# Attention probabilities: scaled with queries on the partitions and transposed, instead of scored a second time transposed

## What is computed

```python
s = jnp.einsum('bqkgd,blkd->bkgql', qblk, k).astype(jnp.float32)
if sink is not None:
    s = jnp.concatenate([s, col], axis=-1)       # one sink logit per head
p = jax.nn.softmax(s, axis=-1)
if sink is not None:
    p = p[..., :-1]
return jnp.einsum('bkgql,blkd->bqkgd', p.astype(v.dtype), v)
```

## Time and profile before

| what | value |
|---|---|
| median of 3 runs | 1517.91 us (1515.63 to 1521.51) |
| profiled execution, its time | 1520.94 us |
| its span (first to last instruction) | 1519.1 us |
| mean granted clock of TensorE | 0.986 |
| TensorE busy | 1445.8 us, 95% |
| VectorE / GpSimd / ScalarE busy | 796.1 / 771.7 / 587.9 us (52 / 51 / 39%) |

### The profile page before, as it was taken

The page is one execution under the profiler, slowest core; times in us unless marked ns, Lnnn a source line. Parts: engine busy times, 40 slices in busy tenths (PEclk is TensorE's granted clock), DMA queues, the critical chain, the costliest instruction groups (busy, mean ns, idle before and its releaser), DMA issues.

```text
span 1519.1 us, 21747 instructions
## 1 busy us (share of the span) xinstructions
PE 1445.8 (95%) x8776; PEld 1306.1 (86%) x8776; DVE 796.1 (52%) x1164; ACT 587.9 (39%) x934; POOL 771.7 (51%) x554
## 2 busy tenths in 40 slices
PE   5999999999998999999979999998999999999996
PEld 3898889889887888999868988897988879999985
DVE  4675676452677520312784747764436775022157
ACT  4334564233764311213243346542357632222140
POOL 2454676323676443344674557753246755443443
PEclk9999999999999999999999999999999999999998
DMA  8412000212000443444320220012110013215221
GB/s 336 126 56 74 29 28 21 90 47 83 28 29 28 132 156 122 141 159 139 124 98 28 88 70 15 29 56 73 56 57 28 29 53 113 76 62 198 96 99 70
DMA packets 36756, 126.90 MB, mean 84 GB/s; under 512 B 5040, under 2 KB 5680, under 8 KB 36656
## 3 DMA queue, kind: packets, MB, share of 16 engines
q1 hardware_dynamic: 29952, 108.54, 21.3%
q10 hardware_dynamic: 6704, 16.97, 3.1%
HBM read 119.73 MB, written 5.77 MB: 83 GB/s over the span
## 4 chain that ended last, share of the span: by engine, by line
PE 87%; DVE 5%; POOL 3%; issue 2%; ACT 2%; DVEq 0%; POOLq 0%; ACTq 0%
PE ps L910 46%; PE ps L858 7%; PE ps L860 7%; PE ps L859 7%; PE ps L1045 3%; PE ps L1043 2%; PE ps L1095 2%; PE ps L1072 2%; PE ps L1071 2%; PE ps L1092 2%; PE ps L1093 2%; PE ps L927 1%; POOL w_lo L1764 1%; DVE o_inv L1633 1%; PE ps L1102 1%
## 5 line engine op out<-in xcount | busy, mean ns | idle before, releaser
L1764 POOL TENSOR_TENSOR w_lo<-raw,w_hi 128x1024 fp32r<-128x1024 f32 x148 | 360.1, 2440 | 359.0 <-ACT w_hi L1138 358.7
L910 PE MATMUL ps<-h_hi,w_hi 128*128 128x320 f32 x1280 | 299.3, 315 | 18.4 <-DVE g_c L1645 8.0
L910 PE MATMUL ps<-h_hi,w_lo 128*128 128x320 f32 x1280 | 292.6, 310 | 0.0
L910 PE MATMUL ps<-h_lo,w_hi 128*128 128x320 f32 x1280 | 292.6, 310 | 0.0
L1792 POOL TENSOR_TENSOR p_lo<-p_f,p_hi 128x512 fp32r<-128x512 f32 x164 | 211.9, 1296 | 139.0 <-ACT p_hi L1298 138.2
L910 PEld LDWEIGHTS ps<-h_hi,w_hi 128*128 128x128 f32 x1280 | 217.3, 189 | 39.3 <-DVE g_c L1645 9.8
L910 PEld LDWEIGHTS ps<-h_lo,w_hi 128*128 128x128 f32 x1280 | 215.9, 189 | 2.2
L910 PEld LDWEIGHTS ps<-h_hi,w_lo 128*128 128x128 f32 x1280 | 215.6, 189 | 2.2
L1138 ACT ACTIVATE w_hi<-raw 128x1024 fp32r<-128x1024 f32 x148 | 152.8, 1051 | 92.1 <-DMA raw<-in_weights 53.7
L1589 DVE TENSOR_REDUCE top<-ps 128x1 f32<-128x512 f32 (+1 forms) x128 | 83.7, 658 | 144.7 <-PE ps L1050 105.0
L1660 DVE TENSOR_TENSOR gy<-ps,sg 128x640 f32<-128x640 f32 x32 | 26.4, 824 | 241.2 <-PE ps L910 241.1
(11 more groups left out here) (180 smaller groups left out, 2599.2 us busy)
## 6 DMA issues: line engine op xcount, KB each, us to landing
raw<-in_weights SPq DMA_DIRECT2D x190, 512.0 KB, 3.4
raw_more<-in_weights SPq DMA_DIRECT2D x10, 512.0 KB, 10.6
x<-in_x_sample ACTq DMA_DIRECT2D x6, 512.0 KB, 8.0
x_mid<-x ACTq DMA_DIRECT2D x5, 512.0 KB, 2.6
x<-x_mid ACTq DMA_DIRECT2D x5, 512.0 KB, 6.5
y_sample<-x SPq DMA_DIRECT2D x3, 512.0 KB, 2.6
pack<-in_pack ACTq DMA_DIRECT2D x2, 528.0 KB, 4.8
x<-in_x_sample SPq DMA_DIRECT2D x2, 512.0 KB, 4.9
```

The lines of the kernel that those rows point to most:

```text
L910: last = pe.matmul(ps[:, s + half, 0:HALF], w[:, u % RING, cols], acts[:, k, half * HALF:(half + 1) * HALF], start=k == 0 and part == 0, s ...
L1764: did(pool.tensor_tensor(w_lo[:, n % RING, :], raw_tile(r), w_hi[:, n % RING, :], ALU.subtract), w_ready)
```

## The change

- The transposed scores, the `row` transposes, `q_m`, the ones rows and the sink's slots and products go.
- `S` stays. When VectorE has a head's maximum it writes at once the negated maximum, joined with the cache's maximum or the sink (`neg`), and a new entry `ex` on ScalarE exponentiates that head's scores from the score bank into `p_f` in SBUF, with the sum of the row taken by the same instruction. The bank is free after `ex`, no longer after the maximum. In A the cached keys' scores are first copied to SBUF (`cached`).
- A new entry `iv` on VectorE adds the partial sums, takes the reciprocal of 128x4 and scales each head's probabilities in place.
- `T` replaces `ST`: TensorE transposes four 128x128 blocks of the scaled probabilities into one bank; ScalarE copies them out rounded (`p_hi`), and VectorE subtracts straight from PSUM (`pl`, formerly GpSimd's).
- `PV` is two products: the value operand holds high and low values side by side, and meets `p_hi` and `p_low`. `O` adds both halves: ScalarE copies the lower half out, VectorE adds.
- `attention` gets a first filler, put between the first scores: z1 and gate b3, which used to be made ahead of the stage. `lag` is 2 instead of 3. Scores of group g begin with the last step of group g - 2, since `p_f` has two buffers, and `iv` comes two steps ahead of the group's first transposes. `with_splits` places no split between a group's last score and its `iv`.
- `zeros` (one memset) takes the place of `ones`.

```diff
-def attention(l, br, filler, last_filler, lag, row_ahead, score_ahead):
+def attention(l, br, first_filler, filler, last_filler, lag, ahead):
...
+        holder = p_place(g)[2]
+        start = -1 if holder < 0 else first[holder + 1] - 1
+        end = max(first[g] - ahead, start)
         for i, e in enumerate(units):
-            early[start + (end - start) * (i + 1) // len(units)].append(e)
+            at = start + (end - start + 1) * i // len(units)
+            scores[at].append(e)
+            exps[at].append(("ex", *e[1:]))
+        inverses[end if end < 0 else end + 1].append(("iv", l, br, g))
...
     for n, (g, i) in enumerate(steps):
-        out.append(("ST", l, br, g, i))
-        out.extend(early[n])
+        out.append(("T", l, br, g, i))
+        out.extend(scores[n])
+        out.append(("pl", l, br, g, i))
         tick()
         if n >= lag:
             product(n - lag)
         fill()
+        out.extend(inverses[n])
+        out.extend(exps[n])
...
-    out.extend(flat(attention(l, "a", filler[:-5], filler[-5:], 3, 2, 4)))
+    out.extend(flat(attention(l, "a", filler[:8], filler[8:-5], filler[-5:], 2, 3)))
...
-    out.extend(flat(attention(l, "b", filler[:-3], filler[-3:], 3, 2, 4)))
+    out.extend(flat(attention(l, "b", filler[:6], filler[6:-3], filler[-3:], 2, 3)))
...
+        if e[0] == "S" and e[4] == len(score_units(*e[2:4])) - 1:
+            held = True
+        if e[0] == "iv":
+            held = False
...
-            while started and turn in due and due[turn] <= 0 and not (freed[turn - RING][:2] == ("oc", 0)):
+            while started and not held and turn in due and due[turn] <= 0 and not (freed[turn - RING][:2] == ("oc", 0)):
...
+                    elif kind == "T":
+                        _, l, br, g, i = e
                         s = begin(e)
+                        n = NO[("iv",) + e[1:4]]
+                        pe.wait_ge(over_sum, n + 1)
+                        for h in range(GRP):
+                            last = pe.transpose(ps[:, s, h * P:(h + 1) * P], p_part(br, g)[:, h, i * P:(i + 1) * P], ident)
                         did(last, filled[s])
...
+                        n = NO[("T",) + e[1:]]
+                        wait_drained(pe, ("T",) + e[1:])
+                        values = vv[:, key, kv, :, :].rearrange("p s d -> p (s d)")
+                        pe.matmul(ps[:, b, :], values, p_hi[:, n % 3, :], start=i == 0, stop=False)
+                        last = pe.matmul(ps[:, b, :], values, p_low(br, n), start=False, stop=ends)
...
+                        for h in range(GRP) if unit == "heads" else (unit,):
+                            p, bias = p_part(br, g)[:, h, :], neg[:, c % 3, h:h + 1]
+                            if br == "a" and unit != "heads":
+                                wait_drained(act, ("S", l, br, g, 0))
+                                act.activation(p[:, LAT * P:], cached[:, g % 2, h * P:(h + 1) * P], ACT.Exp, bias=bias,
+                                               accum_out=sums[:, c % 3, 1, h:h + 1])
+                                p = p[:, 0:LAT * P]
+                            n = p.shape[-1]
+                            src = ps[:, s, h * P:(h + 1) * P] if unit == "heads" else ps[:, s, 0:n]
+                            last = act.activation(p, src, ACT.Exp, bias=bias, accum_out=sums[:, c % 3, 0, h:h + 1])
+                        did(last, drained[s])
...
+                            after(did(dve.tensor_reduce(best[:, h:h + 1], ps[:, s, 0:n * P], axis=AX.X, op=ALU.max)))
+                            other = others[:, h:h + 1] if br == "a" else sinks[:, h:h + 1]
+                            did(dve.tensor_scalar(neg[:, c, h:h + 1], best[:, h:h + 1], other, -1.0, ALU.max, ALU.mult), neg_made)
...
+                        wait_drained(dve, ("S", l, br, g, len(score_units(br, g)) - 1))
+                        total = sums[:, c, 0, :]
+                        if br == "b" or GROUPS[g][1]:
+                            after(did(dve.tensor_tensor(total, total, sums[:, c, 1, :], ALU.add)))
+                        after(did(dve.reciprocal(inv[:, c, :], total)))
+                        for h in range(GRP):
+                            part = p_part(br, g)[:, h, :]
+                            last = dve.tensor_scalar(part, part, inv[:, c, h:h + 1], None, ALU.mult)
+                        did(last, over_sum)
+                    elif kind == "pl":
+                        _, l, br, g, i = e
+                        n, s = NO[e], PLACE[("T",) + e[1:]][0]
+                        dve.wait_ge(p_hi_made, n + 1)
+                        did(dve.tensor_tensor(p_low(br, n), ps[:, s, :], p_hi[:, n % 3, :], ALU.subtract), drained[s])
```

More of the change, by code:

```diff
@@ L42 @@
 FRONT = 0
-TOP_ROW = 96
 HF_ACT = 4
@@ L52, with group_slots, p_place @@
 FIRST_MODS = (0, 4, 1, 5, 2, 6, 3, 7)
-def key_slots(br, tile):
-    last = [(SINK, None)] if br == "b" else []
+def group_slots(br, g):
+    tile = GROUPS[g][1]
     if tile == 0:
-        return [(0, None)] + last
+        return [0]
     if br == "a":
[L62 to L68, removed]
+        return [1, 2, 3, 4, CACHE]
+    return {1: [CACHE, 1, 2], 2: [CACHE, 1, 2, 3], 3: [2, 3, 4, CACHE], 4: [3, 4, CACHE]}[tile]
+def p_place(g):
+    return (g % 2, 0, g - 2) if g < 2 * T - 2 else (0, g - (2 * T - 2), 2 * T - 4)
 def score_units(br, g):
@@ L102, in attention @@
     first = [steps.index((g, 0)) for g in range(count)]
-    early = {n: [] for n in range(-1, len(steps))}
-    start = -1
+    scores = {n: [] for n in range(-1, len(steps))}
+    exps = {n: [] for n in range(-1, len(steps))}
+    inverses = {n: [] for n in range(-1, len(steps))}
     for g in range(count):
         units = [("S", l, br, g, u) for u in range(len(score_units(br, g)))]
-        end = max(first[g] - score_ahead, -1)
+        holder = p_place(g)[2]
+        start = -1 if holder < 0 else first[holder + 1] - 1
+        end = max(first[g] - ahead, start)
         for i, e in enumerate(units):
-            early[start + (end - start) * (i + 1) // len(units)].append(e)
[L110 to L115, removed]
+            at = start + (end - start + 1) * i // len(units)
+            assert at >= -1 and (holder < 0 or at >= first[holder + 1] - 1)
+            scores[at].append(e)
+            exps[at].append(("ex", *e[1:]))
+        inverses[end if end < 0 else end + 1].append(("iv", l, br, g))
     filler = list(filler)
-    places = len(steps) + len(early[-1])
+    places = len(steps)
     out, later, used = [], [], [0, 0]
@@ L289, in layer_order @@
                 ("qt", l, "b", 0)])
-    for c in range(KT_B):
+    for c in range(KT_B - 1):
         out.extend(whole(gate("b", c)))
@@ L293, in layer_order @@
     filler = []
-    for br in "cu":
-        for c in range(KT_B):
-            filler.extend(chunks(gate(br, c), 6))
-            filler[-1] = (filler[-1], gate(br, c))
-    out.extend(flat(attention(l, "b", filler[:-3], filler[-3:], 3, 2, 4)))
+    for br, c in [("b", KT_B - 1), *((br, c) for br in "cu" for c in range(KT_B))]:
+        filler.extend(chunks(gate(br, c), 6))
+        filler[-1] = (filler[-1], gate(br, c))
+    out.extend(flat(attention(l, "b", filler[:6], filler[6:-3], filler[-3:], 2, 3)))
     out.append(("pool", 0, 1, 2, 3, 4, 5, 6, 7))
@@ L393, in with_splits @@
 def with_splits(order, freed, lag):
-    count, out, due, turn, started = len(freed), [], {}, RING, False
+    count, out, due, turn, started, held = len(freed), [], {}, RING, False, False
     for e in order:
@@ L586 @@
 V_HI, O_MADE, O_DONE, MOD_USER = counts()
-ROWS = [e for e in ORDER if e[0] == "row"]
-O_STAGES = [e[:4] for e in ORDER if e[0] == "O" and e[4] == 0]
+NEG_NO = {}
+for _e in [e for e in ORDER if e[0] == "S"]:
+    NEG_NO[_e] = len(NEG_NO) + 1
+ES_NO = {}
+for _e in [e for e in ORDER if e[0] == "S" and e[2] == "b" and score_units(*e[2:4])[e[4]] in ("heads", GRP - 1)]:
+    ES_NO[_e] = len(ES_NO) + 1
+O_STAGES = [e for e in ORDER if e[0] == "O"]
 O_PER_LAYER = len(O_DONE) // DEPTH
@@ L1634, in _ @@
                         for odd in range(2):
[L1635 to L1638 removed]
+                            dve.wait_ge(o_low_made, 2 * n + odd + 1)
+                            half = og_sum(n)[head_rows(odd), :, :]
@@ L1639, in _ @@
+                            last = dve.tensor_tensor(half, by_head(ps[0:HD, b, :])[:, odd:GRP:2, :], half, ALU.add)
+                            did(last, drained[b] if odd else None)
                     elif kind == "gT" and e[2] == "u":
```

279 lines of the change are left out of this document (103 added, 176 removed).

## The result

The changed kernel takes 1553.15 us (median of 4 runs, 1551.52 to 1554.89); the kernel before took 1518.42 beside it (4 runs). The ratio is 1.0228, with a 95% interval of 1.0205 to 1.0251: 35 us slower, where 45 faster was forecast. The mechanism is that of rival 3, GpSimd holding up the scalings. That its 1556 lies so close is partly luck: it had A 17 us and B 2 us longer, and they became 10 to 13 and 4 to 7 us longer.

A forecast was written before the change was run, and what follows sets the result against it. TensorE, busy 95%, was taken as the bound. Savings of 6.2 + 4.7 in the A stages, 2 x 16.2 in B and 1 for the keys make 44.3 us: 1473 us from a median of 1517.9, range 1445 to 1500.

The forecast's parts named there:

- rival 3: Attention stages: GpSimd holds VectorE's scalings through the shared port, 3 us more per group, 1556 us in all; chance 8%.
- TensorE's arithmetic: Attention slots: 0.91 us each instead of 1.175; TensorE alone 57.6 us less over the four stages.
- The 1.0 us per group: VectorE in A: GpSimd's disturbance of five exposed small operations, 0.2 each; bounds 0 and 2.4.
- VectorE level with TensorE in A: Stage A, per group: VectorE 12.0 us, 13.0 with disturbance, against TensorE's 11.8; A about 118.5 us, VectorE above 90% busy.
- Start wait: First transpose of each stage waits for the first group's chain: 2 us idle and 1 of clock per stage.
- g_c handovers: In B, gate products wait for ScalarE's evacuation of g_c: 1 us at each of 8 handovers, 8 us.
- B of layer 1: Taken to repeat layer 0's B: 118 us, 16.2 less in each layer.
- (c): Layer 0's A: first scores wait for the last keys; net 1 us less, bounds +1 and -4.
- the 0.19 us per exponential: ScalarE: extra cost of exponentials that also sum their row, bounded by 0 and 0.19 each, taken as 0.

The follow-up runs named there:

- e1: The changed kernel with weight splits held back until the group's first transposes instead of until its inverse is in the order; 1507.15 us, 0.9922 of the kernel before.
- e4: e1 with the inverse and its scaling placed ahead of the step's low-part subtraction and filler; 1495.43 us, 0.9845 of the kernel before.
- e7: e4 with a step's exponentials put ahead of its filler; 1492.81 us, 0.9822 of the kernel before.
- e8: The changed kernel with each scaling on VectorE also summing its row, a sum nobody reads; 1534.6 us, 1.0108 of the kernel before.

## Why the prediction was wrong

- **TensorE's arithmetic: right.** The slot's own steps: 145.15 to 146.06 is four transposes and two value products, 0.91 us, as worked out from 0.44 and 0.47.

```profile
145.15 0.60 PE L1077 MATMUL ps<-ident_r,p_f_a 128*128 128x128 f32 x4
145.51 0.48 PE L1088 MATMUL ps<-p_hi,vv 128*128 128x512 f32 x1
145.82 0.39 PE L1089 MATMUL ps<-p_lo_a,vv 128*128 128x512 f32 x1
146.06 0.46 PE L925 MATMUL ps<-h_hi,w_hi 128*128 128x320 f32 x2
```

- **The step that failed** is in VectorE's part: "that no split is issued between a group's last score and its scaling keeps the long waits off the four scalings, by the code". The hold ends at the entry `iv`, and an entry of the order is no moment. VectorE reaches it only once ScalarE has made the last exponential, and the split, released behind the next transpose, arrives with it. e1 moves only the end of the hold and brings back 46 of the 80 us of the miss; the place of the inverse behind the low part of its step (e4) is another 12. The 1.0 us per group that was priced (0.2 for each of five small operations) was for operations that mostly were not held up: the negation stays at 212 to 216 ns. The held one was taken as safe.
- **The price of a hit** had two halves. Rival 3 had 3 us per group, all as length; e1 measures 3.4 per hit, half of it clock, for 14 hits. The forecast noted the same pair, a stall and then the lower level, at the earlier trace rows and did not carry it over to new stalls. Rival 3 was right in mechanism, its 8% too little; "for it" stood the 2.636 of the earlier trace rows, an in-place scaling of the same form beside w_lo (all four long ones of that line ran beside one), and "against it" the code's order and the end of p_lo, which freed GpSimd but left w_lo where it was.
- **VectorE level with TensorE in A: wrong in kind.** It is busy 92 us of 123 in e4, not above 90% (the forecast's 112 also held the gaps in its chain, and 1.3 us too much: 0.69 + 0.14 + 0.16 is 0.99, not 1.03, four times in each of 8 groups). What counts is the latency of maximum, exponential, reciprocal, scaling, transpose. Without stalls from hits (e4: the stages from their first score, and the 1 to 2 us of filler ahead of it) A is 125 us (118.5 forecast) and B 124 to 126 (the forecast's 118 plus the 4.6 us its window leaves out, 122.6; some 121 in layer 1). These four differences, some 20 us, are most of what lies between 1473 and e4's 1495; that they come from the chain's length is argued from the waits that are left, and no run takes them apart.
- **Start wait:** 1.0 to 1.1 us at each stage, 2 forecast. **g_c handovers:** 8 us forecast for each B, none in the changed kernel, where waits for the scaling and the score banks (17.5 us) seem to have taken up the slack; once most of these are gone, in e7, 4.7 and 4.6 us for ScalarE, and 2.4 each for VectorE's update. ScalarE evacuates g_c only 4 times in a B, where the forecast counted 8 handovers. **B of layer 1** was taken as a repeat of layer 0's; it was 1.6 us shorter before, so there was less to gain. **(c):** the new wait for the last keys is 1.1 us, at the upper bound given; the rest of the kernel became 3.7 us shorter, 1 forecast, inside its bounds.

Not settled: the clock's share of a single hit. The first hit of B in the changed kernel stalls TensorE for 1.72 us in layer 0 and 1.69 in layer 1, and only in layer 1 does the granted clock fall behind it:

```profile
392.00:400.00 8.00, 5.28 (x32) 4.46 (x31) 7.03 (x13) 3.68 (x10) 2.28 (x3) 1.00 0.18 66
1158.00:1166.00 8.00, 5.31 (x24) 4.45 (x23) 7.30 (x12) 3.06 (x8) 2.88 (x2) 0.79 0.18 68
```

The same lies behind the second A, which is 1.6 us longer than the first with the same hits: it idles 0.9 us less and is busy 2.5 us more, at 0.94 where the first had 0.96. What decides it is open. And no run separates the 0.19 us per exponential (below) from the chain that it lengthens.

## What to carry to other kernels

When a step moves onto a chain with no slack, look for what in the present trace stretches an instruction of exactly that form, and price that case first; one largest value five times the median is the row to believe. A guard written in the order of a list protects a place in the list, not a time: ask which engine reaches the guarded entry late. And a stall of 2 to 3 us on TensorE should be priced about twice on the average, as it was here: once as idle time and once as the slower work behind it.

## What the runs showed of the hardware beyond this

Each exponential that also sums its row is followed by a separate instruction on ScalarE, 224 of them, most at 0.19 us, of which no row of before told; the forecast took the low end of its bound, 0, where the high end, 0.19, was right, and the exponential of 512 columns itself went from 0.598 to 0.68 us. The same kind of instruction on VectorE takes 0.08 us (e8).

```profile
168.38 0.19 ACT L1294 ACTIVATION_READ_ACCUMULATOR p_f_a<-ps,neg 128x1 f32 x1
```
